# Last stage of an encoder block: the product with p in high and low parts, its weights split during the last experts, and two tiles' even rows loaded early

## What is computed

```python
r = DEEPNORM_ALPHA * h + moe_ffn(h, ...)                       # 512 x 1024, 64 experts
r = r + jax.nn.sigmoid(r @ ple_w_gate[i]) * (p[i] @ ple_w_proj[i])   # p: 512 x 256, w_proj: 256 x 1024
h = layer_norm(r, ln2_g[i], ln2_b[i])
```

## Time and profile before

| | us |
|---|---|
| median of 3 runs | 1092.89 |
| lowest and highest run | 1091.17, 1094.14 |
| profiled execution, its own time | 1090.4 |
| span of the profiled execution | 1088.6 |
| PE busy | 1059.9 (97%) |
| DVE busy | 853.4 (78%) |
| ACT busy | 716.7 (66%) |

### The profile page before, as it was taken

How to read it: one execution, slowest core, us unless ns; L and a number is a source line. 1 busy time by engine, 2 the same in 40 slices (tenths; PEclk the granted TensorE clock), 3 DMA queues, 4 the chain that set the end, 5 groups by cost and what they waited for, 6 DMA issues and landing times.

```text
span 1088.6 us, 15813 instructions
## 1 busy us (share of the span) xinstructions
PE 1059.9 (97%) x5382; PEld 864.9 (79%) x5382; DVE 853.4 (78%) x906; ACT 716.7 (66%) x819; POOL 237.1 (22%) x173
## 2 busy tenths in 40 slices
PE   5999999999999999999999999999999999999996
PEld 4778877778888767888888888888888888888585
DVE  6654345663355788999999999999999999999476
ACT  3431244451242527888889988888998888888643
POOL 1000000000005120333333333333333333332101
PEclk9999999999999999999999999999999999999998
DMA  8532221214356449999999999999999999999831
GB/s 296 196 117 78 78 78 39 79 39 155 116 199 237 155 133 347 366 388 391 384 379 384 392 372 392 395 389 388 382 385 374 392 385 390 382 390 342 271 120 61
DMA packets 72571, 294.80 MB, mean 271 GB/s; under 512 B 15312, under 2 KB 18384, under 8 KB 47696
## 3 DMA queue, kind: packets, MB, share of 16 engines
q1 hardware_dynamic: 52944, 256.43, 60.0%
q0 software_dynamic: 19008, 35.71, 12.7%
q10 hardware_dynamic: 576, 2.10, 0.5%
HBM read 283.67 MB, written 44.04 MB: 301 GB/s over the span
## 4 chain that ended last, share of the span: by engine, by line
PE 92%; DMA 3%; DVE 2%; ACT 1%; issue 1%; SPq 0%; DVEq 0%; POOLq 0%; ACTq 0%
PE ps L416 26%; PE ps L418 25%; PE ps L417 25%; PE ps L1562 5%; PE ps L1586 1%; PE ps L1275 1%; PE ps L753 1%; PE ps L777 1%; PE ps L764 1%; DMA residual_rows<-y,put_idx 1%; DMA raw<-in_w_in 1%; DVE w_lo L400 1%; PE ps L325 1%; ACT w_hi L395 1%; PE ps L1546 0%
## 5 line engine op out<-in xcount | busy, mean ns | idle before, releaser
L1825 DVE TENSOR_TENSOR w_lo<-gu_raw,w_hi 128x2048 fp32r<-128x2048 f32 x128 | 292.3, 2284 | 1.0 <-ACT w_hi L1673 1.0
L1673 ACT ACTIVATE w_hi<-gu_raw 128x2048 fp32r<-128x2048 f32 x128 | 245.0, 1916 | 0.0
L416 PE MATMUL ps<-w_hi,xgT_hi 128*128 128x512 f32 x512 | 200.1, 391 | 0.8 <-issue 0.8
L418 PE MATMUL ps<-w_hi,xgT_lo 128*128 128x512 f32 x512 | 199.8, 390 | 0.0
L417 PE MATMUL ps<-w_lo,xgT_hi 128*128 128x512 f32 x512 | 199.2, 389 | 0.0
L1830 DVE TENSOR_TENSOR dn_lo<-dn_raw,dn_hi 128x2048 fp32r<-128x2048 f32 x62 | 142.2, 2293 | 20.8 <-ACT dn_hi L1682 20.8
L416 PE MATMUL ps<-w_hi,act_hi 128*128 128x512 f32 x368 | 146.6, 398 | 0.0
L418 PE MATMUL ps<-w_hi,act_lo 128*128 128x512 f32 x368 | 143.7, 390 | 0.0
L417 PE MATMUL ps<-w_lo,act_hi 128*128 128x512 f32 x368 | 143.4, 390 | 0.0
L1682 ACT ACTIVATE dn_hi<-dn_raw 128x2048 fp32r<-128x2048 f32 x62 | 118.8, 1917 | 0.0
L416 PEld LDWEIGHTS ps<-w_hi,xgT_hi 128*128 128x128 f32 x512 | 96.1, 188 | 21.3 <-issue 1.3
(11 more groups left out here) (218 smaller groups left out, 1763.6 us busy)
## 6 DMA issues: line engine op xcount, KB each, us to landing
gu_raw<-in_moe_w_gate SPq DMA_DIRECT2D x64, 1024.0 KB
gu_raw<-in_moe_w_up SPq DMA_DIRECT2D x64, 1024.0 KB
dn_raw<-in_moe_w_down SPq DMA_DIRECT2D x62, 1024.0 KB
raw<-in_w_in SPq DMA_DIRECT2D x18, 1024.0 KB, 5.2
h_rows<-x_rows SPq DMA_DIRECT2D x8, 512.0 KB, 4.5
raw<-in_w_out SPq DMA_DIRECT2D x4, 1024.0 KB, 4.9
ple_raw<-in_ple_w_gate SPq DMA_DIRECT2D x4, 1024.0 KB, 9.9
x_rows<-in_x SPq DMA_DIRECT2D x4, 512.0 KB, 10.0
```

Of the source, the lines that this page charges most:

```text
L416: nc.tensor.matmul(out, x_hi, w_hi, start=first, stop=False)
L418: return nc.tensor.matmul(out, x_lo, w_hi, start=False, stop=last)
L1673: nc.scalar.activation(m.w_hi[:, 2 * x.b + half], m.gu_raw[:, 2 * x.b + half], ACT.Copy).then_inc(gu_hi, 1)
L1825: nc.vector.tensor_tensor(m.w_lo[:, 2 * x.b + half], m.gu_raw[:, 2 * x.b + half], m.w_hi[:, 2 * x.b + half].bitcast(F32), ALU.subtract).th ...
```

## The change

1. The product with p is made by `product3` from high and low parts: `pT_hi`, `pT_lo` for the turned rows (ACT copy, then a DVE subtraction), `p_w_hi`, `p_w_lo` for the weights. Its eight units go to the banks 2, 7, 5, 6, 0, 1, 2, 7 in place of 0 and 1 in turn. All eight come before the turning of tile 0.
2. SP loads the weights of p where it loaded piece 0 of the gate weights, and piece 0 where it loaded the weights of p. Raw weights of p lie in the 8 KB at 128, piece 0 in those at 192.
3. ACT makes `p_w_hi` after the high part of h(62), ahead of y(61); DVE makes `p_w_lo` ahead of h(63). ACT makes the high part of the turned p ahead of y(62), DVE the low part behind that of h(63).
4. SP loads the even rows of tiles 0 and 1 as soon as the last scatter into `residual_rows` has landed, and then the odd rows of both in a row, ahead of piece 3.
5. The norm's gain and shift are loaded after the last product with p (`p_w_hi` lies where they go).
6. ACT copies unit 0 out before it splits piece 0. DVE adds the rows of tile 1 after the low part of piece 3.

```diff
-        self.pT = at("pT", [P, 2, SEQ], F32, 188)
-        self.p_w = at("p_w", [P, HC], F32, 192)
+        self.pT_hi = at("pT_hi", [P, 2, SEQ], F32R, 188)
+        self.pT_lo = at("pT_lo", [P, 2, SEQ], F32R, 184)
+        self.p_w_hi = at("p_w_hi", [P, HC], F32R, 168)
+        self.p_w_lo = at("p_w_lo", [P, HC], F32R, 128)
+        self.p_w = at("p_w", [P, HC], F32, 128)
...
 # SP, end of the experts
                 sp.wait_ge(gu_lo, 2 * ((r + 1) * NE) - 1 + 2 * LEAD)
+                embedding.load_p_weights(sp)
+                sp.wait_ge(dn_lo, (r + 1) * NE - 2 + LEAD)
                 embedding.load_weights(sp, 0)
-                sp.wait_ge(dn_lo, (r + 1) * NE - 2 + LEAD)
-                embedding.load_p_weights(sp)
...
                 embedding.load_weights(sp, 2)
+                sp.wait_ge(put[0], 16 * ((r + 1) * (NE // 2) + ZEROS[0]))
+                embedding.load_even(sp, 0)
+                embedding.load_even(sp, 1)
...
     def sync(self, sp):
         sp.wait_ge(self.scattered, 1)
-        for t in range(NT):
-            sp.dma_start(m.x[:, t], ...)
-            sp.dma_start(m.x_odd[t // 2][:, t % 2], ...)
-            if t == 0:
-                self.load_weights(sp, 3)
+        self.load_odd(sp, 0)
+        self.load_odd(sp, 1)
+        self.load_weights(sp, 3)
+        for t in range(2, NT):
+            self.load_even(sp, t)
+            self.load_odd(sp, t)
+        sp.wait_ge(self.p_sum, 2 * NT)
...
+    def split_p_weights(self, act):
+        act.wait_ge(self.pw_in, 16)
+        self.nc.scalar.activation(self.m.p_w_hi[:], self.m.p_w[:], ACT.Copy).then_inc(self.pw_hi, 1)
+
+    def low_p_weights(self, dve):
+        dve.wait_ge(self.pw_hi, 1)
+        self.nc.vector.tensor_tensor(m.p_w_lo[:], m.p_w[:], m.p_w_hi[:].bitcast(F32), ALU.subtract).then_inc(self.pw_lo, 1)
+
+    def low_p(self, dve):
+        for pair, bank in enumerate(self.PT):
+            cols = slice(2 * pair * P, 2 * (pair + 1) * P)
+            dve.wait_ge(self.p_turned, 2)
+            dve.wait_ge(self.pT_hi_done, pair + 1)
+            self.nc.vector.tensor_tensor(m.pT_lo[:, :, cols], self.turned_p(bank), m.pT_hi[:, :, cols].bitcast(F32),
+                                         ALU.subtract).then_inc(self.pT_ready, 1)
...
 # PE
-                last = nc.tensor.matmul(ps[:, MAIN[c]], m.pT[:, j, t * P:(t + 1) * P], ...)
+                last = product3(nc, ps[:, self.OUT[u]], m.pT_hi[:, j, rows], m.pT_lo[:, j, rows],
+                                m.p_w_hi[:, cols], m.p_w_lo[:, cols], j == 0, j == 1)
             last.then_inc(self.p_sum, 1)
-            if u == 6:
-                turn(0)
+        turn(0)
```

More of the change, by code:

```diff
@@ L1734, in step @@
                     split_hT(x.next(-1))
+                    with act.If(peak[0] <= (x.r + 1) * CAP):
+                        embedding.split_p_weights(act)
                     scale_y(x.next(-2))
@@ L1738, in step @@
                     split_hT(x)
+                    with act.If(peak[0] <= (x.r + 1) * CAP):
+                        embedding.copy_turned_p(act)
                     scale_y(x.next(-1))
                     put_list(x)
[L1741 to L1742 removed]
                     scale_y(x, bank=XT)
@@ L1864, in step @@
                     split_hT(x.next(-1))
+                    with dve.If(peak[0] <= (x.r + 1) * CAP):
+                        embedding.low_p_weights(dve)
                     times_up(x)
@@ L1867, in step @@
                     split_hT(x)
+                    with dve.If(peak[0] <= (x.r + 1) * CAP):
+                        embedding.low_p(dve)
                     return
@@ L2073, in turn @@
             last.then_inc(self.turned, 1)
[L2075 removed]
+        pe.wait_ge(self.pw_lo, 1)
         for u in range(2 * NT):
             t, c = divmod(u, 2)
[L2078 to L2081 removed]
+            if u in (0, 4):
+                pe.wait_ge(self.pT_ready, u // 4 + 1)
+            if u == 2:
+                pe.wait_ge(self.p_out, 1)
+            if u >= 6:
+                pe.wait_ge(self.p_out, u - 5)
             for j in range(2):
[L2083 to L2085 removed]
+                rows, cols = slice(t * P, (t + 1) * P), slice(j * D + c * 512, j * D + (c + 1) * 512)
+                last = product3(nc, ps[:, self.OUT[u]], m.pT_hi[:, j, rows], m.pT_lo[:, j, rows],
+                                m.p_w_hi[:, cols], m.p_w_lo[:, cols], j == 0, j == 1)
             last.then_inc(self.p_sum, 1)
[L2087 to L2088 removed]
+        turn(0)
         for u in range(2 * NT):
@@ L2138, in high_part @@
                                  ACT.Copy).then_inc(self.hi_done, 1)
+        copy_pp(0)
         ring.split_hi(act, 0)
-        copy_pp(0)
+        copy_pp(1)
         ring.split_hi(act, 1)
-        copy_pp(1)
         copy_pp(2)
+        copy_pp(3)
         ring.split_hi(act, 2)
-        copy_pp(3)
-        copy_pp(4)
-        copy_pp(5)
-        copy_pp(6)
+        for u in range(4, 2 * NT):
+            copy_pp(u)
         high_part(0)
-        copy_pp(7)
         ring.split_hi(act, 3)
```

36 lines of the change are left out of this document (16 added, 20 removed).

## The result

| | us |
|---|---|
| before, median of 6 runs (1091.17 to 1094.14) | 1092.31 |
| after, median of 6 runs (1098.16 to 1103.02) | 1100.03 |
| ratio, 95% interval | 1.0077 (1.0066 to 1.0088) |

The change makes the kernel slower by some 8 us. The forecast was 1096.5 (1092.5 to 1098.5), 3.6 us over the median that it started from: the sign is right, the size is half. The profiled execution of after is the slowest of its six: 1103.02, span 1101.3 against 1088.6. Its loss of 12.7 us is therefore read for its parts, and the parts are sized from a second profile of the same kernel (last experiment) and from the runs.

What follows compares the result with a forecast made beforehand. The prediction took PE's last block of gate products, started by the DMA chain of last scatters and row loads, as the bound. Wait for p's weights +3.3 and late row sum +0.3 gave +3.6 on 1092.89: 1096.5, range 1092.5 to 1098.5.

Steps and rivals of the forecast that it cites:

- What bounds the kernel: Last stage: PE's eight gate products move as a block (40.90 us); its start hangs on the last scatters and row loads.
- The product with p: Ahead of tile 0: 2.8 us less PE work, all under the wait for odd rows, so zero gain on the path.
- Term 1: ACT waits for p's weights ahead of y(61), landing 11.9 us after issue: +3.3 us, ends 0 and +4.6.
- Rival A: The forecast itself: ACT waits for p's weights; 1096.5, or 1095.3 to 1097.9 by 10.5 to 13 us of landing; chance 0.66.
- The even rows early: Odd rows of tile 0 land 4.0 us after the last scatter's landing (T), not 5.1: gain 1.1 us at its turning.
- Even 0 lands at T+1.4: Tile 0's even rows, asked for some 2.2 us before the last scatter lands (T), land 1.4 us after it.
- odd 0 behind them: Tile 0's odd rows, queued behind both early even loads at 1.3 us per half MB, land at T+4.0.
- The contention priced at zero: Early row loads beside the last scatter cost nothing, as their bytes start some 2 us after issue; bound 1 us.
- rival C: Early loads hold up the last scatter, or y(63) waits for expert 61's scatter: 1 to 2 us more, 1098.2; chance 0.11.
- Term 2: PE waits 1.2 us for tile 1's late row sum, giving back tile 0's gain: +0.1 to +0.3 us, ends -1.1 and +1.2.
- The sum: Whole kernel: 3.3 + 0.3 = +3.6 us, from median 1092.89 to 1096.5.
- rival B: Not slower: p's weights land within 8 us of issue, ACT does not wait; 1093.1, chance 0.17.

Runs made afterwards that it cites:

- e17: The changed kernel unaltered, run and profiled again: 1100.62 us, ratio 1.0092 to the kernel before.
- e3: Changed kernel with p's weights split late, row loads and tile 1's sum as before; only the six-bank product is left: 1092.72 us, ratio 1.0012.
- e10: e3, but SP issues nothing behind the odd rows of tile 0 until they have landed; no early loads: 1092.05 us, ratio 1.0008.
- e11: e3 with 6 products that nobody reads ahead of the turning of tile 0: 1091.92 us, ratio 1.0005.
- e4: Changed kernel with 14 products that nobody reads in each of PE's two gaps, all waits and loads kept: 1096.62 us, ratio 1.0044.
- e8: Changed kernel with 14 products that nobody reads in PE's first gap only, ahead of down(62): 1098.67 us, ratio 1.0061.
- e15: e5 with 6 products that nobody reads ahead of the turning of tile 0: 1094.72 us, ratio 1.0018.
- e1: Changed kernel with p's weights split late, behind h(63)'s parts; early loads and late sum of tile 1 kept: 1094.41 us, ratio 1.0025.
- e2: Changed kernel with row loads and row sums as before; the early split of p's weights stays: 1096.2 us, ratio 1.0043.
- e14: e2 with 14 products that nobody reads in PE's first gap: 1097.04 us, ratio 1.0044.
- e5: Changed kernel with p's weights split late and tile 1's sum as before; both early even-row loads kept: 1095.01 us, ratio 1.0032.
- e16: Changed kernel with tile 1's row sum put back ahead of the low part of weights 3: 1100.54 us, ratio 1.0075.
- e12: e5, but SP issues nothing behind the odd rows of tile 0 until they have landed: 1094.18 us, ratio 1.0028.
- e9: e3 with only tile 0's even rows loaded early and nothing issued behind its odd rows until they land: 1091.88 us, ratio 1.0000.

## Why the prediction was wrong

**What bounds the kernel: right chain, but the block did not move as a block.** The waits that grew are those of scatter and row load. "So the eight gate products only move as a block" held from the turning of tile 1 on (50.6 us to the end before, 50.9 in after, 50.7 in e17). It failed for the first of them: from the turning of tile 0 to that of tile 1 it is 8.2 us before and 11.5 in after, because the clock fell ahead of it.

**The product with p: the cover was priced, the gap was not.** "So the gain on the path is zero" held for its own 2.8 us. But the step stopped there. A product that ends earlier leaves PE idle ahead of tile 0 (0.15 us before, 2.50 in e3), and the granted clock fell to 0.5 for the first pass, which took 1.8 us longer in that profile. In the median it is some 1 us (e3 1.0012, e10 and e11 1.0008 and 1.0005; the intervals overlap). The prediction foresaw that PE would idle twice near 1010 to 1014, and asked nothing of the clock there either. No term of the sum was PE's clock; this is the failed step that costs most: some 3.5 us in the changed kernel, by e4, which keeps every wait and load.

**Term 1, the wait for p's weights: right mechanism and place, end of range too near.** 3.3 us, measured 3.2 to 3.5 in four profiles with a landing of 11.0 to 12.1, and 4.9 to 6.9 in three with 13.3 to 14.5. The forecast 11.9 is near the lower end of what this load does; the end of +4.6 came from the longest median in the earlier trace rows, 13.2, and a median is no end. The mean of the seven is 4.4, of which some 0.1 each is e8's unread products and the clock of after. Rival A's times are off by 0.2 and 0.3 us on its own terms: 10.5 and 13 us of landing give 1095.1 and 1097.6, not 1095.3 and 1097.9.

**The even rows early: wrong sign.** Forecast was a gain of 1.1 us, with the odd rows at T+4.0; measured T+6.3 to T+6.6 in eight profiles and T+5.9 in e15, a loss of 0.7 to 1.4 against the kernel before. Two steps failed. "Even 0 lands at T+1.4" took the 3.6 us of a load in an empty queue; beside the last scatter it landed at T+2.7 to T+3.8. And "odd 0 behind them" put a half MB more ahead of the one load that the chain waits for, at a price of 1.3 each, as if the first had been paid before T. The contention priced at zero was most of the term. Its reason, bytes that start some 2 us after the issue, is not borne out: in the kernel before the bytes of the first row load start 1.0 us after it (issued at 1023.57, nothing until 1024.5). The bounds were too tight: rival C named the mechanism only for the scatter, which was not held up (4.40 against 4.68), and y(63) of after waited for PE and not for the scatter of expert 61.

**Term 2, the late row sum: near nothing, as forecast, but not for its reason.** The +0.1 to 0.3 was a gain of 1.1 at tile 0 given back by a wait of PE. There was no gain, and the wait came only where the clock was kept (e4), 0.2 us; in the changed kernel PE arrived later than the sum. That this term's size was right is luck.

**The sum.** By the profile of e17, which is the mildest: +3.4, +1.3, +2.0, with 0.3 ahead of y(60), is the 7.0 us of its span over that of before. By the runs, the product alone with its fallen clock is 0.12% (e3; 1.3 us), and over it the early split 0.31% (e2, e14; 3.4), the early loads 0.20% (e5; 2.2): 6.9 us, of 8.4 measured at first (7.2 to 9.6) and 10.0 in e17 (8.4 to 11.6). What is left is some 1.5 to 3 us. The clock behind the first gap would fit, 0.16% between after and e8: the mean clock is 0.990 to 0.994 in the 16 executions of after, e16 and e17, and 0.993 to 0.995 in those of e5, e8 and e12, in which only the second gap is open. How often the clock fell at the first gap isn't known beyond the profiles (it did in after and e16, not in e17), so this part stays open.

The fit of the Trainium skill that the prediction named beside rival B (DMA: Bandwidth & Descriptors, Anatomy of one DMA, 2.0 us plus bytes over 436 GB/s) gives by estimate 4.4 us for 1 MB and 3.2 for a half. The page has it per DMA, for those that POOL issues; p's weights are issued by SP behind other loads, and took 11.0 to 14.5 us, 2.5 times the estimate and more. Where the queue was empty it came near: the first half MB of rows took 3.6 us in the kernel before, and the odd rows 4.41 in e10, behind a half MB and with nothing after them.

## What to carry to other kernels

Work that is off the critical path may be made shorter, but look at what PE does in the time won: if it idles just ahead of the block that sets the end, the block may start at half the clock. Then look at the granted clock of every execution and not of the profiled one alone. A load moved early beside another transfer is not paid for early; count the bytes that stand ahead of the load that the chain waits for, from the moment at which that chain starts. A copy that waits for a load must not stand in an engine's queue ahead of work that the chain needs: here the same split a few instructions later cost little (y(61) to y(62) is 7.34 to 7.36 us in all eleven profiles with the late split, 7.16 before).

## What the runs showed of the hardware

- The same 1 MB load at the same place of the queue took 11.0 to 14.5 us to land in seven profiles.
- A half MB load with 1 MB ahead and nothing behind took 6.06 us, in the last two of which the DMA engines were busy for 0.14 and then 0.03 of the time (e12).
- The granted clock fell to 0.5 after gaps of PE from 1.40 us, and held at 1.00 after gaps of up to 2.29; in no profile did it hold after 2.77 (the first gap of e16) or more. After short gaps one and the same kernel shows both (e9, e10, e3, e2). The Trainium skill (TensorE: Matmul & The Clock Gate, Part 1) has the array at 1.2 GHz after idle time and 2.4 GHz under work; the rows agree with the two levels.
